# Trunk step with sixteen experts: gate and up pieces of an expert in a row, down pieces of its predecessor behind them

## The reference, cut to what matters

```
cap = CAPACITY_FACTOR * L // N_EXPERTS        # 64 latent rows, 16 context rows
aff = softmax(x @ w_router); g, idx = top_k(aff^T, cap)
xs = x[bidx, idx]                             # 80 rows per expert
h = silu(xs @ w_gate[e]) * (xs @ w_up[e])     # 80 x 1024
y = (h @ w_down[e]) * g
out = zeros.at[idx].add(y)                    # 16 experts
```

## Time and profile before

| what | value |
|---|---|
| median of 3 runs | 2411.11 us |
| the profiled execution's own time | 2412.53 us |
| its span | 2410.7 us |
| PE busy | 2270.8 us, 94% |
| mean granted clock of PE | 0.978 |
| eight gate and up pieces of expert 0 | 1358.5 to 1408 us of the span |
| phases of experts 1 to 15 | 1411.55 to 2373.4 us |
| DMA read and written | 602.75 MB, 24.44 MB |

### The profile page before, as it was taken

One profiled execution on the slowest core, in us unless ns is written; L12 is line 12 of the kernel. 1 busy time (PEld: TensorE's weight loads), 2 busy tenths in 40 slices (PEclk: granted clock), 3 DMA queues, 4 the chain that ended last, 5 costly groups with the idle time before them and its releaser, 6 DMA issues.

```text
span 2410.7 us, 57295 instructions
## 1 busy us (share of the span) xinstructions
PE 2270.8 (94%) x25884; PEld 1504.0 (62%) x25884; DVE 712.6 (30%) x1167; ACT 477.0 (20%) x1005; POOL 589.1 (24%) x644
## 2 busy tenths in 40 slices
PE   5999999999999999999998589999999999999997
PEld 3468888666566665644455576677676666666763
DVE  4124432367767775311246200000000000000001
ACT  3011111365655654210022000000000000000000
POOL 0246771466666673000300100000000000000000
PEclk9999999999999999999997699999999999999999
DMA  9922222864665654240334789999999999999995
GB/s 371 364 81 63 83 54 67 216 212 152 199 207 179 198 188 150 99 151 25 150 140 190 290 317 397 409 408 410 409 413 412 420 409 410 409 408 393 408 415 191
DMA packets 182973, 630.81 MB, mean 262 GB/s; under 512 B 13002, under 2 KB 89508, under 8 KB 152324
## 3 DMA queue, kind: packets, MB, share of 16 engines
q1 hardware_dynamic: 164224, 587.07, 63.4%
q0 software_dynamic: 3328, 20.97, 3.3%
q10 hardware_dynamic: 15188, 19.19, 2.4%
HBM read 602.75 MB, written 24.44 MB: 260 GB/s over the span
## 4 chain that ended last, share of the span: by engine, by line
PE 71%; DMA 14%; DVE 6%; issue 4%; ACT 2%; POOL 1%; SPq 1%; ACTq 1%; DVEq 0%; POOLq 0%
PE PS L1567 19%; PE PS L1477 12%; PE PS L1386 11%; PE PS L1581 9%; DMA work<-in_w_gate 9%; PE PS L1200 8%; DMA hT_<-in_w_gate 3%; PE PS L1142 3%; PE PS L1077 3%; POOL work L2165 1%; DVE PS L1917 1%; PE PS L1372 1%; PE PS L1104 1%; DMA work<-in_w_ada 1%; DVE work L1876 1%
## 5 line engine op out<-in xcount | busy, mean ns | idle before, releaser
L1567 PEld LDWEIGHTS PS<-hT_,work 128*64 128x64 f32 x14336 | 510.1, 139 | 93.6 <-issue 75.6
L1567 PE MATMUL PS<-hT_,work 128*64 128x80 f32 x14336 | 529.4, 235 | 36.4 <-issue 26.1
L1386 PE MATMUL PS<-hT_,work 128*128 128x512 f32 (+1 forms) x1536 | 433.2, 434 | 0.0
L2165 POOL TENSOR_TENSOR work<-work 128x512 f32<-128x512 f32 x240 | 305.4, 1273 | 167.7 <-ACT work L971 152.1
L1386 PEld LDWEIGHTS PS<-hT_,work 128*128 128x128 f32 x1536 | 226.4, 192 | 146.9 <-issue 146.8
L1581 PE MATMUL PS<-work,hT_ 128*32 128x512 f32 (+1 forms) x2544 | 299.9, 596 | 3.1 <-DMA work<-in_w_down 2.8
L2029 DVE TENSOR_TENSOR hT_<-PS,hT_ 128x480 f32<-128x480 f32 x16 | 10.5, 658 | 933.3 <-ACT hT_ L1060 933.3
L1477 PE MATMUL PS<-work,mixT_ 128*128 128x512 f32 x640 | 282.5, 602 | 0.0
L2219 POOL DMA_INDIRECT out_y<-mixT_,work x16 | 23.4, 1461 | 795.3 <-DVE mixT_ L2047 795.3
L1477 PEld LDWEIGHTS PS<-work,mixT_ 128*128 128x128 f32 x640 | 122.9, 194 | 150.8 <-issue 150.8
L1200 PE MATMUL PS<-work,hT_ 128*128 128x256 f32 x960 | 214.4, 382 | 0.5 <-DMA work<-in_w_in 0.5
(11 more groups left out here) (266 smaller groups left out, 1854.0 us busy)
## 6 DMA issues: line engine op xcount, KB each, us to landing
work<-in_w_up SPq DMA_DIRECT2D x57, 2048.0 KB, 27.2
work<-in_w_down SPq DMA_DIRECT2D x56, 2048.0 KB, 33.7
work<-in_w_gate SPq DMA_DIRECT2D x55, 2048.0 KB, 32.2
work<-in_w_ada SPq DMA_DIRECT2D x48, 2048.0 KB, 9.7
work<-in_w_in SPq DMA_DIRECT2D x80, 512.0 KB, 5.9
hT_<-in_w_gate SPq DMA_DIRECT2D x9, 2048.0 KB
work<-in_w_out SPq DMA_DIRECT2D x4, 4096.0 KB, 13.5
hT_<-in_w_down SPq DMA_DIRECT2D x8, 2048.0 KB
```

Of the source, the lines that this page charges most:

```text
L1386: last = pe.matmul(qk_bank(which)[:, (ctx_at if ctx_ else lat_at)[which]], w_chunk[chunk % NW][:, HD * (k % 8):HD * (k % 8) + HD], hT[:, k ...
L1567: last = pe.matmul(hidden_at(u, f)[64 * h:64 * h + 64, :], w[:, k % 4, f // 2, f % 2, 64 * h:64 * h + 64], xsT[s][:, k, :], start=opens, s ...
L2165: TT_(acc_ctx[p % 3], acc_ctx[p % 3], prod[i % 3], ALU.add).then_inc(s_padd, 1)
```

## The change

`ORDER` becomes the plain order 0 to 11, so the ring holds the eight gate and up pieces of an expert and then the four down pieces of its predecessor. With the ring's order equal to PE's order, `used_up_to(r)` is r + 1, and the count at which the gate and up part of an expert is done is 12e + 4 (eight pieces into the phase, which begins at 12e - 4). In `expert` the eight `gate_up` calls stand in a row, the `turn_four` calls keep their places behind j = 1, 3, 5, 7, and the eight `down` calls of e-1 follow. Expert 0, the last four down pieces, ACT, DVE and POOL keep their code; only the count from `done_gate_up` changes for ACT and DVE.

```diff
-        ORDER = [0, 1, 8, 2, 3, 9, 4, 5, 10, 6, 7, 11]
-        USED = [0, 1, 3, 2, 4, 6, 5, 7, 9, 8, 10, 11]
+        ORDER = [0, 1, 2, 3, 4, 5, 6, 7, 8, 9, 10, 11]
 
         def used_up_to(r):
 
-            return r + 1 if r < 8 else r - (r - 8) % 12 + USED[(r - 8) % 12] + 1
+            return r + 1
...
-            return 8 if isinstance(e, int) and e == 0 else 12 * e + 7
+            return 8 if isinstance(e, int) and e == 0 else 12 * e + 4
...
-                for j in range(9):
-                    if j < 8:
-                        gate_up(s, j, r0 + ORDER.index(j), rounds)
-                    if j:
-                        down(e - 1, 1 - s, j - 1, r0 + ORDER.index(8 + (j - 1) // 2), rounds)
+                for j in range(8):
+                    gate_up(s, j, r0 + j, rounds)
                     if tokens is not None and j % 2 == 1:
                         if j == 1:
                             pe.wait_ge(s_gath[1 - s], tokens)
                         turn_four(e + 1, 1 - s, j // 2)
+                for k in range(8):
+                    down(e - 1, 1 - s, k, r0 + 8 + k // 2, rounds)
```

## The result

The changed kernel takes 2490.14 us (median of 4 runs, 2488.46 to 2501.4) against 2411.83 us (median of 4, 2406.52 to 2415.27) before: a ratio of 1.0335, 95% interval 1.0313 to 1.0356. It is slower by 78 us; forecast were 2501 us, within 2457 to 2541.

A forecast was written before the change was run, and what follows sets the result against it. Transfers set the pace before; after the change PE with its instruction fetch would. Per phase 39.0 + 10.3 + 20.8 = 70.1 us, times 15 = 1051.5 against 961.9 us: +89.6 on 2411.1, say 2501 us, range 2457 to 2541.

The forecast's parts named there:

- The resource: Gate and up rows: PE's instruction fetch, blocks of 256 every 6.37 us against 4.80 us of work a block.
- No waits for weights: Expert stage: PE's waits for weights go away altogether, since PE with its fetch sets the pace.
- none inside the down calls: Eight down calls in a row: 384 instructions in 20.8 us need at most 1.5 blocks, so no gap.
- unchanged packets on the instruction queue: Profile page after: the instruction queue still has about 203 packets.
- Rival A: Expert stage: the fetch stays hidden and transfers set the pace, 6 us gained, 2405 us; chance 0.05.
- B: Expert stage: gaps also make the granted clock fall, once a phase 36 us, 2537 us; chance 0.12.
- The down calls in a row: Each phase's eight down calls together: 20.8 us instead of 21.7, a gain of 0.9 us a phase.
- The gap term: Gate and up row: second border about 0.7 us, the other 6.1 cost 1.57 us each, 10.3 us a phase.
- The first border: Start of each gate and up row: its block is already in place after the down calls, so no gap.
- Rival C: Gate and up row: more held ahead, first three borders free, 8.0 us of gaps a phase, 2466 us; chance 0.15.
- The work term: PE's work in each phase: 39.0 us for pieces and transposes plus 20.8 us for down calls.
- the pace of the fetch: Period of 256-instruction blocks, read from expert 0: 6.37 us; 6.0 us would give 2467 us, 6.7 us 2531.

The follow-up runs named there:

- e1: Changed kernel, with only 512 of 4096 columns loaded of every weight piece behind the first eight; 2335.22 us, ratio to the kernel before 0.9684.
- e2: Kernel before the change, with the same cut to 512 of 4096 columns of every weight piece behind the first eight; 2347.88 us, ratio 0.974.
- e7: Changed kernel, with only 2048 of 4096 columns loaded of every weight piece behind the first eight; 2382.25 us, ratio to the kernel before 0.9887.
- e5: Changed kernel, with gate and up pieces arriving in runs of 4 KB instead of 16 KB, same bytes; 2491.0 us, ratio to the kernel before 1.0334.
- e3: Changed kernel, with one matmul on each 128x128 weight tile instead of two on its halves; 2803.83 us, ratio to the kernel before 1.1625.
- e4: Kernel before the change, with one matmul on each 128x128 weight tile instead of two on its halves; 2797.47 us, ratio 1.1601.
- e6: Kernel before the change, with gate and up pieces in runs of 4 KB instead of 16 KB; 2421.42 us, ratio 1.0046.

## Why the prediction was right

*The resource.* The gaps named "issue" 128 matmuls or a multiple of it apart, taken from the eight pieces of expert 0, came out in all phases. No waits for weights, none inside the down calls, unchanged packets on the instruction queue: as forecast. Rival A (transfers decide, 2405 us) is out. B (the clock falls once a phase or more) came true in small part: five falls of 3.4 us in 15 phases. In the fall at 1778.8, 127 matmuls take 6.29 us instead of 4.6, so one costs about 1.7 us; an estimate from that is 8 us in all at most, not 36.

*The down calls in a row.* Forecast 0.9 us a phase. The timeline of e1 shows it: eight calls in 20.74 us (1801.63 to 1822.37) against 8 x 2.71 = 21.7. Pieces in a row save a little too, which the prediction left out: two of them take 9.01 us (1842.12 to 1851.13) instead of 9.16. With what gaps are left in e1, its stage is 0.8 us a phase shorter than that of e2: 896.5 us (1400.72 to 2297.17) against 908.4 us (1398.40 to 2306.80).

*The gap term* was too large: 10.3 us a phase forecast. The rows call 120.7 + 1.1 us idle in 15 phases, 8.1 us each, but that is a smaller measure than the prediction's, which took periods from start to start. A matmul's row lasts 0.23 us with a modelled end, while the next normally starts 0.036 us after it, so each gap hides some 0.2 us. From start to start, less that normal distance, the pauses sum to about 140 us in the trace, 9.3 us a phase. The price of one was right, 1.49 us on the mean against 10.3 / 7.1 = 1.45. Their number was not: 94 in 15 phases, 6.3 each, where the prediction has 7.1. The first border is free, as forecast; the second is the first to cost in ten phases only, and seven later ones cost nothing.

*Rival C* (the first three borders free, 5.1 gaps, 8.0 us, 2466) holds in one phase, the one shown above. As a rule it is out, but the truth lies between it and the forecast: 9.3 us of gaps, between 8.0 and 10.3.

*The work term* was good: forecast 59.8 us, and the 1040.8 us less these pauses are 60.0 us a phase. By the idle times of the rows it would look like 61.3, and the kernel before like 61.7 (PE busy 925.87 us) for 60.6 us of pieces, calls and transposes; most of that surplus is the hidden part of the pauses, and the clock's falls can account for the rest, which was not shown apart. With light traffic both orders come down to 59.8 and 60.6, gaps included. So 70.1 us a phase were forecast and 69.4 measured, 10.7 us in all; another 2.4 us came from ahead of the stage, which began at 1409.13 instead of 1411.55.

*What I had wrong in the mechanism.* I took 6.37 us as the pace of the fetch and allowed 6.0 us at best "beside a DMA that is less full". The step rested on expert 0, where the DMA share was 0.84, and I read this as "not full", so as a sign that traffic does not matter. e1 shows a pace under 4.8 us at a share of 0.27; there the gaps of expert 0 are gone too. In that the forecast had luck: it held because the changed kernel keeps the traffic at 0.99, a condition that it did not name, and it would have failed for a stage with few transfers, where this order is the better one. By the sentence of the Trainium skill ("Runtime: NRT & Kernel Launch", "Instruction fetch mechanics"), crossing a block border is mostly hidden: the traces of e1 (5.8 us in 14 gaps) and e2 (none) agree, the changed kernel's, beside 386 GB/s of transfers, does not.

## What to carry to other kernels

Count the instructions as well as the work: where an engine runs many short instructions, look for gaps named "issue" that come at a fixed count, and set the time that the engine needs for so many instructions against the time between them. Such a limit belongs to the order of the work; long instructions put between short ones give the fetch time, and grouping like with like takes it away, even if it saves a little at each change of kind. Before moving a pattern's price to another place, ask which other load was on when it was measured, and take it away once: one run with an eighth of the transfers told apart what a whole profile could not.

## What the runs showed of the hardware

- PE's instructions came in packets of 16 KB, 256 instructions. Beside full weight traffic they started 5.8 us or more apart in the kernel before and 4.35 us or more in the changed one (median 6.4 in both), with an eighth of the traffic down to 3.4 us (e1). The gaps grow with the share of traffic (e7 lies between), do not change with the length of the gate and up packets (e5), and they do not go by the number of packets (e1). The packet itself took about 1 us each time. Whether it matters how many transfers are queued is not shown: from 1850 to 2110 a piece landed 29.9 to 36.5 us after its issue before the change (medians) and 9.4 to 15.2 us after it, but before the change PE waited for a block in 23 places only.
- The granted clock can stay at its lower level while PE's rows are busy almost throughout: 231 us in e3 (1355.8 to 1587.1), 148 us in e4 (1356.6 to 1504.6), with pieces of 13.8 us instead of 7.5; it rose within 5 us of the first down call.
- With two float32 matmuls on the 128x64 halves of each weight tile, 80 columns each, a piece takes 4.58 us; with one on the whole tile it takes 7.5 us for the same work (e3), both at the upper level of the clock. Splitting the tile was worth 1.6 times, at the price of twice the instructions, and so of the limit that this case is about.
- In the old order, gate and up weights in runs of 4 KB instead of 16 KB moved 4% fewer bytes in the same stretch (e6, 96.99 against 100.90 MB in 260 us).
